# A two-layer encoder step on one core: MLP groups in pairs on TensorE and written out on VectorE, squares of two norms on ScalarE, sums of blocks in a tree

## What is computed

```python
x = x + concat(A, B, C, D of rms_norm(x, g_mix) @ w_in) @ w_out     # four kinds of attention
x = x + square(relu(rms_norm(x, g_mlp) @ w_up)) @ w_down            # 2048 -> 8192 -> 2048
x = x + (ple @ w_ple) * sigmoid(rms_norm(x, g_ple) @ w_ple_gate)    # 2048 -> 2048
```

## Time and profile before

| | us |
|---|---|
| median of 3 runs | 3606.41 (3603.99 to 3607.7) |
| profiled execution, its own time | 3609.22 |
| span of its instructions | 3607.4 |
| TensorE matmul busy | 3385.7 (94%) |
| GpSimd busy | 1899.8 (53%) |
| VectorE busy | 1417.3 (39%) |
| ScalarE busy | 1124.7 (31%) |

### The profile page before, as it was taken

How to read it: one execution, slowest core, us unless ns; L and a number is a source line. 1 busy time by engine, 2 the same in 40 slices (tenths; PEclk the granted TensorE clock), 3 DMA queues, 4 the chain that set the end, 5 groups by cost and what they waited for, 6 DMA issues and landing times.

```text
span 3607.4 us, 58666 instructions
## 1 busy us (share of the span) xinstructions
PE 3385.7 (94%) x20676; PEld 3048.7 (85%) x20676; DVE 1417.3 (39%) x2287; ACT 1124.7 (31%) x1614; POOL 1899.8 (53%) x1189
## 2 busy tenths in 40 slices
PE   7998988999999999999879998889999999999988
PEld 5776755699999999999867776556999999999988
DVE  5334544474052240425352344445630613305163
ACT  2333322332333333332333332223333333333322
POOL 4554200077667666676565541002766676766764
PEclk9999998899999999999989999989999999999999
DMA  5333322144454444444343333222444444444433
GB/s 165 103 111 104 116 59 74 58 145 152 141 150 151 143 149 152 139 152 146 112 143 112 114 93 112 58 68 92 140 151 142 147 152 141 152 143 150 152 120 120
DMA packets 295722, 453.09 MB, mean 126 GB/s; under 512 B 36336, under 2 KB 111344, under 8 KB 294832
## 3 DMA queue, kind: packets, MB, share of 16 engines
q1 hardware_dynamic: 295328, 448.66, 39.3%
q0 software_dynamic: 144, 0.87, 0.1%
HBM read 435.54 MB, written 14.06 MB: 125 GB/s over the span
## 4 chain that ended last, share of the span: by engine, by line
PE 84%; DVE 7%; issue 4%; ACT 2%; DMA 1%; SPq 1%; POOL 0%; DVEq 0%; ACTq 0%; POOLq 0%
PE ps L687 19%; PE ps L686 19%; PE ps L685 19%; PE ps L783 5%; PE ps L746 5%; PE ps L749 4%; PE ps L771 4%; PE ps L748 3%; PE ps L852 1%; DVE ssq L1355 1%; DMA ring<-in_w_in 1%; ACT prob L1120 1%; PE ps L821 1%; PE ps L887 1%; DVE xhi L1305 1%
## 5 line engine op out<-in xcount | busy, mean ns | idle before, releaser
L649 POOL TENSOR_TENSOR wlo<-ring,whi 128x1024 fp32r<-128x1024 f32 x600 | 1479.7, 2468 | 1285.7 <-ACT whi L1105 1285.7
L1105 ACT ACTIVATE whi<-ring 128x1024 fp32r<-128x1024 f32 x600 | 635.0, 1060 | 1420.6 <-PE ps L687 1420.6
L685 PE MATMUL ps<-xhi,wlo 128*128 128x320 f32 x2560 | 802.0, 313 | 23.8 <-issue 17.0
L686 PE MATMUL ps<-xlo,whi 128*128 128x320 f32 x2560 | 797.0, 311 | 0.0
L687 PE MATMUL ps<-xhi,whi 128*128 128x320 f32 x2560 | 796.6, 311 | 0.0
L687 PE MATMUL ps<-hhi,whi 128*128 128x320 f32 x2176 | 674.6, 310 | 0.0
L685 PE MATMUL ps<-hhi,wlo 128*128 128x320 f32 x2176 | 662.4, 304 | 5.9 <-DVE plel L1628 5.9
L686 PE MATMUL ps<-hlo,whi 128*128 128x320 f32 x2048 | 629.8, 308 | 0.0
L636 POOL TENSOR_TENSOR rlo<-ring,whi 128x256 fp32r<-128x256 f32 (+2 forms) x576 | 416.4, 755 | 378.2 <-ACT whi L1089 378.0
L685 PEld LDWEIGHTS ps<-xhi,wlo 128*128 128x128 f32 x2560 | 486.3, 190 | 29.2 <-issue 27.5
L686 PEld LDWEIGHTS ps<-xlo,whi 128*128 128x128 f32 x2560 | 486.2, 190 | 1.0 <-issue 0.4
(11 more groups left out here) (240 smaller groups left out, 3253.0 us busy)
## 6 DMA issues: line engine op xcount, KB each, us to landing
ring<-in_w_up SPq DMA_DIRECT2D x256, 512.0 KB, 3.7
ring<-in_w_down SPq DMA_DIRECT2D x256, 512.0 KB, 3.5
ring<-in_w_in SPq DMA_DIRECT2D x120, 512.0 KB, 3.5
ring<-in_w_out SPq DMA_DIRECT2D x64, 512.0 KB, 3.9
ring<-in_w_ple_gate SPq DMA_DIRECT2D x64, 512.0 KB, 3.5
xsave<-x SPq DMA_DIRECT2D x8, 640.0 KB, 7.8
x<-xsave SPq DMA_DIRECT2D x8, 640.0 KB, 5.0
ring<-in_w_in SPq DMA_DIRECT2D x16, 288.0 KB, 2.8
```

What stands on the lines that cost most here:

```text
L649: nc.gpsimd.tensor_tensor(wlo[:, s, :], ring[:, s, :], whi[:, s, :].bitcast(f32), ALU.subtract)\
L685: mm(out, lo[:, k, cols], xh, start=start, stop=False)
L686: mm(out, hi[:, k, cols], xl, start=False, stop=False)
L1105: A(whi[:, s, :], ring[:, s, :], ACT.Copy).then_inc(hi_ready, 1)
```

## The change

1. TensorE's loop over four MLP groups becomes a loop over two pairs, with both groups of a pair in its body. VectorE's loop over groups is written out four times.
2. At the layer's start ScalarE squares x, four blocks (128x1280) at a time, one piece after each of units 4 to 7. At the gate it does so after the halves of the four `w_ple` units, into `hid`. VectorE no longer does these two squarings. The squaring before the MLP stays on VectorE.
3. In all three norms VectorE's TENSOR_REDUCE is replaced by four adds of halves: 2560, 1280, 640 and 320 elements a partition.

```diff
-                with pe.Fori(0, FG) as g:
+                with pe.Fori(0, FG // 2) as pair:
+                  for group in range(2):
+                    g = 2 * pair + group
                     for c in range(4):
                         gemm_chunk(l, Q_MLP + 16 * g + 2 * c, ...
@@ ScalarE, layer start
-                halves(l, range(4, 11))
+                for q in range(4):
+                    halves(l, (4 + q,))
+                    A(plout[:, 4 * q:4 * q + 4, :], x[:, 4 * q:4 * q + 4, :], ACT.Square).then_inc(first_squared, 1)
+                halves(l, range(8, 11))
@@ ScalarE, gate
-                for i in range(9):
+                upper_halves(l, Q_PLE)
+                act.wait_ge(half_free, l * CHUNKS + 2 + 4 + 8 * FG)
+                for b in range(0, KB, 4):
+                    A(hid[:, b:b + 4, :], x[:, b:b + 4, :], ACT.Square).then_inc(gate_squares, 1)
+                for i in range(1, 9):
                     upper_halves(l, Q_PLE + i)
@@ VectorE
+            def add_blocks(sq16):
+                for n in (8, 4, 2):
+                    done(add(sq16[:, 0:n, :], sq16[:, 0:n, :], sq16[:, n:2 * n, :]))
+                return add(acc[:, 0:TOK], sq16[:, 0, :], sq16[:, 1, :])
             def first_squares(l):
-                done(mul(plout, x[:, :, :], x[:, :, :]))
-                done(V.tensor_reduce(acc[:, 0:TOK], plout.rearrange("p b t -> p t b"), X, ALU.add))
+                dve.wait_ge(first_squared, (l + 1) * 4)
+                done(add_blocks(plout))
                 V.tensor_copy(acc[:, TOK:], acc[:, 256:TOK]).then_inc(acc_ready, 1)
             def squares_pass(l, chunks):
                 done(mul(hid[:, :, :], x[:, :, :], x[:, :, :]))
-                V.tensor_reduce(acc[:, 0:TOK], hid[:, :, :].rearrange("p b t -> p t b"), X, ALU.add).then_inc(acc_ready, 1)
+                add_blocks(hid).then_inc(acc_ready, 1)
@@ VectorE, MLP
-                with dve.Fori(0, FG) as g:
+                for g in range(FG):
@@ VectorE, gate
-                squares_pass(l, 4 + 8 * FG)
+                dve.wait_ge(gate_squares, (l + 1) * 4)
+                add_blocks(hid).then_inc(acc_ready, 1)
```

More of the change, by code:

```diff
@@ L193, in build @@
         sq_ready = sem("sq_ready")
+        gate_squares = sem("gate_squares")
+        first_squared = sem("first_squared")
         ssq_ready = sem("ssq_ready")
@@ L1633, in _ @@
                 squares_pass(l, 4)
-                UP_STEPS = 2 * KB - 4
-                with dve.Fori(0, FG) as g:
-                    here[0] = l * STEPS + g * UP_STEPS
-                    at0 = count[0]
+                for g in range(FG):
                     dve.wait_ge(rms_ready, l * N_RMS + g + 2)
@@ L1654, in _ @@
                                             ALU.subtract).then_inc(hid_ready, 1)
-                    assert count[0] - at0 == UP_STEPS
                     for c in range(4):
                         add_chunk(l, MLP0 + 32 + 64 * g + 8 * c, 8 + 8 * g + c, c % 2, 4 * c)
-                here[0] = l * STEPS
-                count[0] += (FG - 1) * UP_STEPS
                 gain_blocks = 0
```

## The result

The changed kernel takes 3578.5 us (median of 4 runs, 3575.4 to 3586.3) where the kernel before took 3607.1 beside it: a ratio of 0.9919, 95% interval 0.9907 to 0.9932. That is 0.8% faster, 24 to 34 us. The forecast was 3577.3 us.

The account below looks back on a forecast made before the run. TensorE's matmuls fill nearly the whole span, so only its gaps can be won. Terms 19.5 + 6 + 4.5 - 0.3 - 0.6 = 29.1 us gave a median of 3577.3 us, range 3564 to 3588 (0.8).

Parts of the forecast that it names:

- loop over pairs, four jumps: TensorE's MLP loop: four jumps back go, each saving its gap and the half clock after it, 19.5 us (13.6 to 21).
- VectorE's loop: MLP groups on VectorE: writing the loop out costs nothing, since VectorE waits most of each group for TensorE.
- gates, with the stretch to the layer's end: Gate sum in each layer: shorter sum, partly lost to delayed splits; 3 us a layer, 6 in all (-2 to +17).
- start of the second layer: Second layer's start: without the mul GpSimd's low half comes earlier, so TensorE waits less; 4.5 us gained (1.5 to 7.3).
- start of the first layer: First layer's start: no gain, as the load was late; the collision on unit 7 costs 0.3 us.
- before the MLP: Norm before the MLP: the tree ends later by turns with GpSimd, costing 0.3 us a layer, 0.6 in all.
- The signs named ahead: Profile: four branches, two issue gaps (6.8 us), 1.27 us squares, sum wait 2 to 6.5, new copy wait, second-start gap 1.2.
- pairs don't save a jump's cost: MLP loop: the inner seam stalls as well, so only 9 us or less remains, 3597 to 3606; chance 0.04.
- The slower rival: TensorE's MLP waits: one more register instruction at each of 512 units costs 43.5 us, 14 slower, 3621; chance 0.05.
- the count of GpSimd's instructions in reach: Gate tree: two GpSimd instructions of 2.3 us stand between the adds, making 5.6 us into 10.2.
- rival about the gate: Two rivals: the gate gives nothing (3590, chance 0.19), or VectorE slips between GpSimd's instructions (3562, chance 0.17).
- the collision on unit 7: Second layer's start: unit 7's low-half pieces on GpSimd wait for the tree's adds, so TensorE waits some 2.5 us.

Follow-up runs that it names:

- experiment 4: The kernel before with only VectorE's loop over the groups written out: 3608.4 us, ratio 1.0000 to the kernel before.
- experiment 1: The kernel before with TensorE's loop over pairs and VectorE's loop written out, mul and reduce kept on VectorE: 3584.8 us, ratio 0.9940.
- experiment 8: The changed kernel with TensorE written out wholly, no loop over pairs or layers: 3566.7 us, ratio 0.9890 to the kernel before.
- experiment 3: The changed kernel with VectorE's reduce kept in all three sums in place of the tree: 3574.8 us, ratio 0.9917 to the kernel before.
- experiment 5: The changed kernel with the first gate unit's first high half made between ScalarE's second and third square: 3576.2 us, ratio 0.9914 to the kernel before.
- 7: The kernel before with ScalarE's squares alone, reduce and loops as before: 3598.9 us, ratio 0.9973 to the kernel before.
- experiment 2: The changed kernel with both group loops as before, so ScalarE's squares and the tree alone: 3602.9 us, ratio 0.9983 to the kernel before.
- experiment 10: The changed kernel with the reduce in place of the tree and TensorE without loops: 3564.5 us, ratio 0.9888 to the kernel before.
- the last one: The changed kernel with the reduce, TensorE without loops and the first gate half made between ScalarE's squares: 3560.6 us, ratio 0.9863 to the kernel before.

## Why the prediction was right

The total and the parts, each in the order of the prediction's terms (us gained, after against before, by the table of events):

| term | forecast | trace |
|---|---|---|
| loop over pairs, four jumps | 19.5 | 23.0 |
| VectorE's loop | 0 | 0 (experiment 4) |
| gates, with the stretch to the layer's end | 6 | 3.8 |
| start of the second layer | 4.5 | 4.7 |
| start of the first layer | -0.3 | -0.5 |
| before the MLP | -0.6 | -0.9 |
| attention, unchanged code | - | +3.7 |

Without the attention the terms make 30.1 where 29.1 were forecast. That the sum came so near is partly luck: the loop gave 3.5 more than its term and the gates 2.2 less, and the two errors nearly cancel. The signs named ahead all showed: four branches, two "issue" gaps of 7.0 us, squares of 1.26 us with none waiting at the gate, the wait for the gate's sum, the new wait for the copies, and 1.13 us at the second start.

**Loop over pairs: right mechanism, size too small by 3.5 us.** The measured 23.0 lies beyond the term's own upper end of 21. The term took the half clock for 2.9 us, from one jump, which is the mildest of the six and one of the two that stay. At the other jumps of the same trace it lasts up to 5.8. TensorE after each of the six jumps of before (stretch, length, busy time and count by engine, granted clock, DMA share, GB/s); the second and the fifth are the jumps that stay:

```profile
981.92:986.12 4.20, 4.20 (x18) 4.20 (x19) 0.00 (x0) 0.00 (x0) 0.00 (x0) 0.59 0.45 129
1211.31:1214.21 2.90, 2.90 (x11) 2.90 (x12) 0.00 (x0) 0.00 (x0) 0.27 (x1) 0.50 0.48 121
1440.48:1446.28 5.80, 5.80 (x22) 5.80 (x23) 0.00 (x0) 0.00 (x0) 0.24 (x1) 0.50 0.34 101
2761.65:2767.55 5.90, 5.90 (x23) 5.90 (x24) 0.00 (x0) 0.00 (x0) 0.15 (x1) 0.52 0.34 96
2992.10:2995.90 3.80, 3.80 (x16) 3.80 (x17) 0.00 (x0) 0.00 (x0) 0.20 (x1) 0.56 0.54 149
3221.58:3224.88 3.30, 3.30 (x13) 3.30 (x14) 0.00 (x0) 0.00 (x0) 0.17 (x1) 0.53 0.55 148
```

What a stretch loses is its length times one minus its clock: 1.7, 2.9, 2.8 and 1.6 us for the four that went, 9.0. Their gaps are 3.64, 3.37, 3.45 and 3.44, 13.9. The sum, 22.9, is what the seams gained (23.0). The rival "pairs don't save a jump's cost" is refuted by experiments 1 and 8: neither the inner seam nor straight code shows a gap. From the reciprocal of one group to the next it is 224.25 us over an inner seam, where it was 229.2 to 230.5 over a jump. The slower rival, arithmetic at every unit, is refuted by the table: from the last group's reciprocal to the first `plout` copy, seven of the group's eight chunks with no seam among them, both kernels take the same 194.06 us, and so does the one that computes no register on TensorE (experiment 8).

The Trainium skill says, in "Runtime: NRT & Kernel Launch", section "Instruction fetch mechanics", that a taken branch to code outside the small window of fetched instructions waits for a DMA. The traces agree as far as they go: in the MLP the gap stands at jumps back only, written-out code has none, and exits take 83 ns. One of the profile's queues for instructions (q8) moved 184 packets before, 179 with four of TensorE's jumps gone (experiment 1 and the changed kernel) and 168 in the kernel without loops; with VectorE's loop alone written out it stayed at 184 (experiment 4). So looped code moved more packets than the same code written out, which fits a fetch at each jump. That the 5 us are this fetch was not tested apart.

**Gate: right way, 2.2 us too much.** Splits and tree were both off. The first gate chunk came 3.20 us late (forecast 3.5). The chain of splits, forecast up to 4.1 later and in the chosen 3 us taken partly recovered, fell back into its rhythm almost wholly: 39.9 us from first copy to the mul before, 40.2 to the tree after, 0.4 later. The tree took 11.86 us, not 10.2, since three GpSimd instructions came between and not two. So 14.34 (mul and reduce) - 11.86 - 0.39 = 2.09 us, and the reciprocal shows 2.10. The rest of the term, -0.6 and +0.2, lies between the gate and the end of the layer. The step of this term that failed is the count of GpSimd's instructions in reach: two, from the units that TensorE finishes. In its undisturbed rhythm (experiment 3) they begin 0.2, 3.8 and 7.3 us behind the start of the sum: three. With two in reach the tree does take 9.8 us (experiment 5), near the 10.2 of the sum. Neither rival about the gate came true: it gave more than nothing, and VectorE didn't slip between GpSimd's instructions, which would have given 17.4 us for both. The wait for the sum, forecast at 2 to 6.5 us, is 6.06.

The rule of the Trainium skill, "SBUF — State Buffer", section "Who interferes with whom", spoke against the tree, and the trace agrees: TENSOR_REDUCE leaves GpSimd's 2.41 us alone (experiment 3), two-operand adds do not (11.33 for three). Keeping the reduce is worth 2.5 to 3.5 us a gate (experiment 3 against the change, 7 against 2). The prediction weighed it as a length of this tree, not as a rival kernel with the reduce. That kernel gains more at the gates, though by time it can't be told from the changed one.

**Start of the second layer: right.** VectorE's and TensorE's timelines after:

```profile
1828.56 6.32 DVE L1281 TENSOR_TENSOR arena<-arena 128x2560 f32<-128x2560 f32 x3 [11.54 <-ACT arena L1199]
...
1821.49 0.47 PE L748 MATMUL ps<-rlo,xw 128*128 128x512 f32 x1 [1.13 <-POOL rlo L638]
1834.59 0.47 PE L748 MATMUL ps<-rlo,xw 128*128 128x512 f32 x1 [1.93 <-POOL rlo L638]
```

The gap of 5.55 us is 1.13 (forecast 1.2), the tree waits for the last square, and the collision on unit 7 costs 1.93 (forecast 2.5). What the prediction hadn't seen is that the layers' own jump costs here as well: without it the start came 2.6 and 3.2 us earlier with the tree (experiment 8), and 2.0 with the reduce (experiment 10 against 3).

**Before the MLP: right.** The tree ends 14.2 us behind the mul (14.8 forecast), where the reduce took 9.6:

```profile
762.54 11.50 DVE L1281 TENSOR_TENSOR hid<-hid 128x2560 f32<-128x2560 f32 x3
774.07 2.59 DVE L1281 TENSOR_TENSOR acc<-hid 128x320 f32<-128x320 f32 x1
```

The four adds of 5.6 us are stretched by GpSimd's turns. TensorE's own arrival hides most of it: the lead falls by 0.3 and 0.6 us here, and by 0.0 and 0.2 with the reduce (experiment 3).

**Attention** is what no term covers. From the first reciprocal to the end of attention, code that none of the edits touches takes 660.5 to 673.4 us over the traces of this study, with no pattern by edit: 668.0 and 660.5 in the two layers of before, 662.6 and 662.3 after, 673.4 and 665.8 in experiment 2 (whose profiled execution was the slowest of its eleven, 11 us above their median), 665.2 and 671.7 in the last one. So nothing shows the +3.7 to be a gain of the change. The forecast's range has to leave room for that alone.

What stays open is how one gets the gate's sum earlier. Neither a later nor an earlier start of the splits moved the tree's start by more than 0.4 us. The timelines suggest that VectorE and GpSimd, waiting for each other through 16 blocks, pace the 40 us from the first copy; this was not shown, as no kernel here took it apart.

## What to carry to other kernels

An operation that would be faster alone is not faster beside a neighbour that it excludes: four adds of 5.6 us by their elements took 7.3 us at the layer starts, 9.8 to 12.0 at the gates and 14.1 before the MLP, while the reduce of 8.8 never took more than 9.6. So the second half of the change won by moving the squares to ScalarE, where they kept their 1.26 us, and not by the tree. A hardware jump on a full TensorE is priced by its gap and by the half clock after it at each place, not by the mildest one, and it pays to write out every jump where no other wait covers it, the layers' too. When an early part of a chain is sped up, look for the pace that the chain falls back into before counting the gain at its end.

## What the runs showed of the hardware

- The half clock (1.2 GHz) after a gap of nearly the same length, 3.3 to 3.6 us, lasted 2.9 to 3.4 us at four jumps and 5.7 to 5.8 at two; at two of the six of before the clock stood at its full level for 0.2 to 0.5 us first and fell only then.
- GpSimd's 16 pieces of 256 columns, which at 2.78 us for four would take 11 us by themselves, took 20.97 against a mul and a tree and 15.33 against a mul and a reduce, and three instructions of 1024, 7.2 us by themselves, took 11.33 against a tree.
- ScalarE's squares of 128x1280 took 1.256 us each, 4.74 for four in a row, without any load of tables ahead of them. The four pieces at the layer's start fitted between its copies.
- The same code took up to 2% longer in one place and execution than in another (attention, 660.5 to 673.4 us). The granted clock over the stretch was 0.92 in the longest of the second layer and 0.93 in the shortest.
